# A two-layer hybrid decoder step on one core: each layer begins with tile 0's queries and keys

## What is computed

```python
def layer(x, h0, buf_a, buf_b, S0, pos, l):
    u = rmsnorm(x, norm_mix_g[l])
    a_gate, a_x, b_in, c_q, c_k, c_v, c_g = jnp.split(u @ w_in[l], splits, axis=-1)
    xa, nbuf_a = causal_dwconv(a_x, buf_a, lru_conv_w[l], lru_conv_b[l])        # 4 taps
    ha, h_last = rglru(xa, h0, ...)                                             # gates from xa
    out_a = gelu(a_gate) * ha
    glu = b_in[..., :W_B] * sigmoid(b_in[..., W_B:])
    cb, nbuf_b = causal_dwconv(glu, buf_b, cm_dw_w[l], cm_dw_b[l])              # 31 taps
    out_b = silu(layernorm_f32(cb, cm_ln_g[l], cm_ln_b[l]))
    q = rope(c_q, pos); k = rope(c_k, pos) * HD_C ** -0.5
    o, S_last = retention(q, k, c_v, S0, 128)
    out_c = silu(c_g) * groupnorm(o)
    x = x + concat([out_a, out_b, out_c]) @ w_out[l]
    return x + hier_moe(rmsnorm(x, norm_ffn_g[l]), ...)
```

## Time and profile before

| | before |
|---|---|
| timed executions | 874.23 us median, 871.57 to 878.54 |
| the profiled execution | 870.6 us, span 868.8 us |
| TensorE busy | 824.2 us, 95% |
| VectorE | 473.3 us, 54% |
| ScalarE, GpSimd | 175.6 us, 139.7 us |
| moved by DMA | 260.06 MB, mean 299 GB/s |
| chain that ended last | PE 79%, DMA 9%, DVE 5%, issue 4% |

### The profile page before, as it was taken

One profiled execution on the slowest core, in us unless ns is written; L12 is line 12 of the kernel. 1 busy time (PEld: TensorE's weight loads), 2 busy tenths in 40 slices (PEclk: granted clock), 3 DMA queues, 4 the chain that ended last, 5 costly groups with the idle time before them and its releaser, 6 DMA issues.

```text
span 868.8 us, 13634 instructions
## 1 busy us (share of the span) xinstructions
PE 824.2 (95%) x5302; PEld 469.0 (54%) x5302; DVE 473.3 (54%) x1099; ACT 175.6 (20%) x361; POOL 139.7 (16%) x193
## 2 busy tenths in 40 slices
PE   7999999999988899999899999999999879999995
PEld 6745554675545455455377445447655545545552
DVE  2468997262212377675624789954421215767666
ACT  2304123301121111111311221232112111111113
POOL 0101030011212222221010001300121113113110
PEclk9999999999999999999999999999999999999998
DMA  9890973669999999999973048347699999999961
GB/s 283 231 359 9 377 213 67 246 207 400 415 419 414 412 416 402 415 413 400 322 254 146 1 167 221 101 103 298 234 403 416 417 415 415 413 403 415 413 264 55
DMA packets 104487, 260.06 MB, mean 299 GB/s; under 512 B 34088, under 2 KB 67900, under 8 KB 87978
## 3 DMA queue, kind: packets, MB, share of 16 engines
q1 hardware_dynamic: 94954, 247.00, 75.3%
q0 software_dynamic: 7680, 9.39, 3.2%
q10 hardware_dynamic: 1792, 2.84, 0.9%
HBM read 265.22 MB, written 15.18 MB: 323 GB/s over the span
## 4 chain that ended last, share of the span: by engine, by line
PE 79%; DMA 9%; DVE 5%; issue 4%; SPq 1%; ACT 1%; POOL 0%; DVEq 0%; POOLq 0%; ACTq 0%
PE psum L1059 20%; PE psum L756 13%; PE psum L1085 11%; PE psum L735 7%; PE psum L681 6%; DMA ring<-in_moe_w 5%; PE psum L925 5%; PE psum L1114 3%; DMA rows<-xn_scratch,sg 3%; PE psum L1108 2%; PE psum L767 2%; PE psum L687 2%; DVE uT L1298 1%; PE psum L1099 1%; PE psum L1000 1%
## 5 line engine op out<-in xcount | busy, mean ns | idle before, releaser
L1059 PE MATMUL psum<-ring,arena 128*64 128x256 f32 x1984 | 227.8, 382 | 6.5 <-issue 4.6
L1059 PEld LDWEIGHTS psum<-ring,arena 128*64 128x64 f32 x1984 | 142.1, 137 | 77.5 <-issue 16.8
L1085 PE MATMUL psum<-ring,arena 128*64 128x512 f32 x496 | 118.2, 604 | 12.4 <-issue 9.0
L756 PE MATMUL psum<-ring,uT 128*128 128x512 f32 x256 | 113.0, 595 | 0.0
L1788 DVE SCALAR_TENSOR_TENSOR arena<-arena,psum 128x128 f32<-128x128 f32 x64 | 18.3, 286 | 115.9 <-ACT arena L2114 102.3
L1780 DVE TENSOR_TENSOR arena<-psum,gff 128x512 f32<-128x512 f32 x64 | 43.7, 687 | 65.6 <-PE psum L681 63.8
L756 PEld LDWEIGHTS psum<-ring,uT 128*128 128x128 f32 x256 | 47.7, 190 | 55.3 <-issue 54.5
L1085 PEld LDWEIGHTS psum<-ring,arena 128*64 128x64 f32 x496 | 36.2, 138 | 71.1 <-issue 70.0
L1834 DVE TENSOR_TENSOR x<-x,psum 128x512 f32<-128x512 f32 x80 | 51.5, 684 | 41.0 <-PE psum L1114 31.5
L2095 ACT ACTIVATE arena<-psum,sg 128x512 f32<-128x512 f32 x64 | 44.0, 688 | 128.4 <-PE psum L1085 126.1
L735 PE MATMUL psum<-uT,ring 128*128 128x288 f32 x256 | 63.1, 407 | 1.0 <-DVE uT L1298 1.0
(11 more groups left out here) (313 smaller groups left out, 912.4 us busy)
## 6 DMA issues: line engine op xcount, KB each, us to landing
ring<-in_moe_w SPq DMA_DIRECT2D x186, 1024.0 KB, 19.4
ring<-in_w_in SPq DMA_DIRECT2D x24, 1024.0 KB, 11.7
ring<-in_w_out SPq DMA_DIRECT2D x8, 1024.0 KB, 7.7
y_scratch<-in_w_out SPq DMA_DIRECT2D x1, 2304.0 KB, 18.8
arena<-in_state_ret SPq DMA_DIRECT2D x16, 128.0 KB, 5.9
out<-arena SPq DMA_DIRECT2D x16, 128.0 KB, 2.5
xn_scratch<-rows ACTq DMA_DIRECT2D x4, 512.0 KB, 3.7
uT<-in_moe_w SPq DMA_DIRECT2D x2, 1024.0 KB
```

Source lines behind the costliest of these rows:

```text
L756: i = pe.matmul(b, uTk[:, k, 128 * t:128 * t + 128], w[:, :, k, :], start=k == 0, stop=k == KT - 1)
L1059: i = pe.matmul(b[64 * j:64 * j + 64, 0:FE], xsT[:, u // 2, k, s], w[j][:, k, :], start=k == 0, stop=k == KT - 1, skip_group_check=True)
L1085: i = pe.matmul(b[64 * q:64 * q + 64, :], hT[:, q, f, :], w[:, 512 * j:512 * j + 512], start=f == 0, stop=f == 1, skip_group_check=True)
```

## The change

Each layer now begins with tile 0 alone: norm of tile 0, q0 on TensorE, and the norms of tiles 1 and 2 run beside it. Then states, (layer 0) parameters, k0, tq0, b4, tk0, b5, b6, b7 and last b0 to b3. SP loads the granules in that order, and the first experts' weights after b3 instead of b5. On VectorE the short convolution moves behind 12 taps of the long one, the samples' taps behind the first rotations; parameters stand between the rotations of q0 and k0. At a layer's end tile 0's sums come first, and the next layer's first tile (or the final norm's) is done ahead of the samples' sums, inside the branch; TensorE no longer waits for the last sums ahead of its branch.

```diff
-WAIT_NORM, WAIT_CHOICE, WAIT_MARKS, WAIT_GATES, WAIT_ROWS = (13, 8), 16, 6, 7, 7
+WAIT_NORM, WAIT_CHOICE, WAIT_MARKS, WAIT_GATES, WAIT_ROWS = (6, 5), 16, 6, 7, 7
...
             for l in range(DEPTH):
-                full(sp, l, "b5")
+                full(sp, l, "b3")
                 expert(l, 0, 0)
...
-                    for kind, u, gs in (("h", 0, (0, 1)), ("h", 1, (3, 4)), ("h", 2, (6, 7)), ("y1", 0, (2, 5))):
+                    for kind, u, gs in (("h", 1, (4, 3)), ("h", 2, (6, 7)), ("y1", 0, (5, 2, 0, 1))):
...
+                norm(l, 0, 0)
                 project("q0", 4, 0)
+                norm(l, 0, 1)
+                norm(l, 0, 2)
+                states(l)
+                if l == 0:
+
+                    pe.wait_ge(param_in, 16 * len(params))
...
                 project("k0", 6, 0)
+                turn("tq0", 0)
+                freed(pe, l, "n1t2a")
+                block(4)
+                turn("tk0", 0)
+                for c in (5, 6, 7, 0, 1, 2, 3):
+                    block(c)
                 project_samples()
...
-                    for a in (0, 2, 1, 3):
+                    for a in range(4):
                         xfreed(pe, f"y{a % 2}", 1, GROUPS - 1, l)
...
                 n = pe.value_load(ovi[0:1, 8:9], min_val=0, max_val=OVER)
-                for kind, u in (("x0", 1), ("x1", 1), ("h", 3), ("hT", 3), ("y0", 1), ("y1", 1), *((f"back{a}", 1) for a in range(5))):
-                    xfreed(pe, kind, u, GROUPS - 1, l)
                 with pe.If(n > 0):
...
+                if l == 0:
+                    dve.wait_ge(const_in, 16)
                 rotate_q(0)
+                if l == 0:
+                    parameters()
                 rotate_k(0)
-                taps(0, 9)
+                glu()
+
+                full(dve, l, "tq0")
+                taps_samples(0)
+                taps_samples(1)
+                own.wait()
+                dve.sem_inc(sample_conv, 1)
+                taps(0, 12)
+                short_conv()
...
-                given_back(NPAIR - 1, (0, 2, 1, 3, 4))
+                given_back(NPAIR - 1, (0, 1))
...
-                    dve.nop()
...
+                    given_back(NPAIR - 1, (2, 3))
+                    first_tile(l + 1)
+                    given_back(NPAIR - 1, (4,))
```

More of the change, by code:

```diff
@@ L724, in _, with project, block @@
             for l in range(DEPTH):
-                for t in range(3):
-                    norm(l, 0, t)
-                freed(pe, l, "n1t2a")
-                for c in range(8):
+                def project(name, g, t):
+                    for h in range(2):
+                        granule(pe, l, g + h, "in")
+                    b = start(l, name)
+                    w = ring[:, g:g + 2, :].rearrange("p g (k c) -> p g k c", k=KT)
+                    for k in range(KT):
+                        if name == "q0" and k % 4 == 0:
+                            freed(pe, l, ("n1t0a", "n1t0b")[k // 4])
+                        i = pe.matmul(b, uTk[:, k, 128 * t:128 * t + 128], w[:, :, k, :], start=k == 0, stop=k == KT - 1)
+                    done(i, name)
+                def block(c):
                     granule(pe, l, c // 2, "in")
                     b = start(l, f"b{c}")[:, 0:NT]
+                    if l == 0 and c == 7:
+                        pe.wait_ge(prm_ready, 1)
                     w = ring[:, c // 2, :].rearrange("p (k c) -> p k c", k=KT)
@@ L858, in _ @@
                 gates("gi1", 1, 1)
-                turn("tq0", 0)
-                turn("tk0", 0)
                 project("q1", 4, 1)
@@ L1359, in _, with short_conv @@
-                dve.wait_ge(glu_ready, 2 * l + 2)
+                def short_conv():
+                    freed(dve, l, "b3")
+                    freed(dve, l, "sa")
+                    last = [None] * 4
+                    for k in range(CONV_A):
+                        for c in range(2):
+                            w = P_(l, "cw", 2 * k + c)
+                            for i, (src, dst) in enumerate((
+                                    (axp[:, c, k:k + SEQ], pr(XA)[:, c, :]),
+                                    (axs[:, c, :, k:k + DT], sa(XA)[:, c, :, :]))):
+                                if k == 0:
+                                    ins_ = S(dst, src, w, P_(l, "cb", c), ALU.mult, ALU.add)
+                                else:
+                                    own.wait(last[2 * c + i])
+                                    ins_ = STT(dst, src, w, dst, ALU.mult, ALU.add)
+                                if k < CONV_A - 1:
+                                    last[2 * c + i] = own(ins_)
+                                elif (c, i) == (1, 1):
+                                    ins_.then_inc(xa_ready, 1)
+                                else:
+                                    own(ins_)
@@ new lines, in glu @@
+                def glu():
+                    freed(dve, l, "b7")
+                    freed(dve, l, "sc")
+                    STT(glp[:, :, 30:LB], pr(xc[:, :]), 1.0, pr(cb[:, :]), ALU.add, ALU.mult).then_inc(glu_ready, 1)
+                    dve.wait_ge(glu_ready, 2 * l + 1)
+                    for c in range(2):
+                        i = STT(gls[:, c, :, 30:LT], sa(xc[:, :])[:, c], 1.0, sa(cb[:, :])[:, c], ALU.add, ALU.mult)
+                        if c:
+                            i.then_inc(glu_ready, 1)
+                        else:
+                            own(i)
+                    dve.wait_ge(glu_ready, 2 * l + 2)
@@ L1517, in _ @@
                 dve.sem_inc(mixa_done, 1)
-                taps(12, 15)
+                taps(15, 18)
                 full(dve, l, "S0")
@@ L1525, in _ @@
                 mask_scores(2)
-                taps(15, 24)
+                taps(18, 25)
                 mask_scores(1)
@@ L1884, in _ @@
                 n = dve.value_load(ovi[0:1, 8:9], min_val=0, max_val=OVER)
[L1885 to L1886 removed]
                 with dve.If(n > 0):
+                    given_back(NPAIR - 1, (2, 3, 4))
+                    for a in range(5):
+                        xfreed(dve, f"back{a}", 1, GROUPS - 1, l)
                     with dve.Fori(0, n) as j:
```

205 lines of the change are left out of this document (86 added, 119 removed), and 1 row of the table jobs.

## The result

The changed kernel takes 879.59 us (median of 17 runs, 874.38 to 888.42), the kernel before, run beside it, 875.17 (17 runs, 870.65 to 878.54): ratio 1.0051, 95% interval 1.0031 to 1.007. That is 4.4 us slower, within the 1% that I had called no change, 5.2 us above my number of 874.4 and inside the range of 868 to 882. The profiled execution took 878.43 us with a span of 876.6, against 868.8 before, so the two traces lie 7.8 us apart.

What follows compares the result with a forecast made beforehand. TensorE was taken as the bound. Layer 0 +2.1 + 1.3, layer 1 -3.3 + 1.3 and end +0.1 gave +1.5 us; on 872.9, the middle of four executions, that made 874.4 us, range 868 to 882.

Steps and rivals of the forecast that it cites:

- The bound: Whole kernel: TensorE, busy 95% of the span, sets the time; gains or losses ahead of the experts' part carry through unchanged.
- Rival 4: Experts' part: the weight stream sets the pace and swallows any shift ahead of it, 0 +- 1 us, 874; chance 0.05.
- Layer 1's head: Start of layer 1: q0 starts 5.3 us sooner, 1.95 of transposes are paid back, net gain 3.3 us.
- Layer 0's head: Start of layer 0: no gain from the new order; low clock and the key's late rotation lose 2.1 us by q1.
- 3.6 us per MB: Loads at layer 0's start: rate from 2.62 MB in 9.6 us, putting granule 5's arrival at 12.2, say 12.5.
- The rotation of k0: Layer 0, VectorE: delayed by constants and parameters, kr done at about 35.2, and TensorE's tk0 waits for it until 35.7.
- the clock term: q0 of layer 0: the first stretch runs at the lower clock, so about 1.7 us falls into q0; bounds 0 and 6.9.
- The wait at the gates: Ahead of gr0, both layers: GpSimd's gelu slows VectorE's taps by 2.3 us, slack 1.0, so TensorE waits 1.3 us each.
- rival 3: At gr0: GpSimd holds up every tap and the short convolution, wait 3.7 us per layer, sum +6.3, 879; chance 0.18.
- Rival 2: At the gates: taps slip between GpSimd's operations without loss, no waits, sum -1.1 or to -4, 870 to 873; chance 0.27.
- The end: Kernel's end: tile 0's last normalisation moves ahead, tile 2's sums behind it; the last tile decides, +0.1 us.
- the edits that I took as free: Six tap instructions done earlier and the first experts' weights loaded after b3 instead of b5: both claimed to cost nothing.

Runs made afterwards that it cites:

- The fastest kernel: Nine ahead-taps instead of 12; layer 0 starts with blocks b4 to b7, has 26 filler passes, b3 between k0 and tq0: 868.12 us, 0.9924 of the kernel before.

## Why the prediction was right or wrong

**The bound** held. What TensorE gained or lost in a head or at the gates arrived at the end: 7.9 at layer 0's q1, 7.9 at the last give-back, 7.8 in the span. Rival 4, the weight stream that swallows a shift, is out. But single traces are not that exact: from q1 of layer 0 to the last give-back the kernels before and after take 360.9 us both, and the traces of experiments whose edits do not touch that part 360.9 to 363.2.

**Layer 1's head** was right: 5.5 us sooner against 5.3, 1.9 paid back against 1.95, net 3.6 against 3.3. That the cover by q0 is what earns it, is shown by the run that takes it away. Reading the overflow count put VectorE's third sum back by 0.4 us, as I had allowed, and cost nothing: the rows of tile 0 were ready at 440.96, and the filler held TensorE until 441.02.

**Layer 0's head** was mis-sized: +3.9 (without the gates) against +2.1. Two terms of it had the right size, transposes 1.9 and clock 1.6 (I had 1.7). Two failed. q0 started at 13.4 rather than 12.5; the arrival of granule 5 varies from 12.2 to 14.6 between profiled runs, and my 3.6 us per MB lies at the early end. And b4 waited 1.35 us for granule 2, a wait that I had not written down. My own figure would have shown it: q0 and k0 use four granules in 14 us, and at 3.6 us per MB they also arrive in some 14, with constants, states and x between them. The rotation of k0, which I had expected to release tk0, did not: it was done at 35.7 (I had "kr at about 35.2", though my terms add up to 34.9), tk0 started at 37.39, and without b4's wait TensorE would have come to it at 36.0, still behind the rotation. The reason that I gave for the clock term was wrong although its size was right: with the cold start removed q0 was as slow (8.80 us), so it goes with the idle time ahead of q0.

**The wait at the gates** had the right place, cause and layer count, and the wrong price: 4.0 and 3.8 us against 1.3 each. I had VectorE late by 1.3, measured is 2.36. The share that a GpSimd operation takes from the taps, "70%", was right: 2.45 us, 69% of the 3.56 that the gelu's operations took. Missing were 0.9 us in the short convolution (5.35 us where 4.5 are usual). 0.8 of them went in the instruction beside L2231, the scaling of the keys, which I had nowhere; GpSimd's copies, which I had in rival 3, took 0.1. And I had no term for what an idle TensorE does to its own clock, 1.7 us in layer 0 and 1.4 in layer 1, though I had priced a low clock in layer 0's head. It is the largest miss, 3.1 of the 6.3 us by which the traces differ from my sum. On the rule that I weighed there (the Trainium skill, "SBUF — State Buffer", Who interferes with whom): that a vector instruction with two SBUF inputs and a GpSimd instruction that reads SBUF exclude each other agrees with the copy of 0.43 us that took 3.44 beside the taps; the loss of the whole of GpSimd's time that I drew from it does not, the taps lost 69% of it.

**The rivals.** Rival 3, to which I gave 0.18, comes nearest: slower, by the wait at the gates. Its 879 against the 879.59 measured is luck. It had a wait of 3.7 in each layer, and measured are 2.36 of wait and 1.4 to 1.7 of clock, which it lacked; it had no larger loss in layer 0's head; and it stood on a time before of 872.9. Rival 2 is refuted by the taps of 11.24 us.

**The end** cost nothing (the last give-back of layer 1 comes 8.0 us later than before, the span is 7.8 longer; I had +0.1), and nothing shows a price of the edits that I took as free: between layer 0's q1 and the last give-back, and again between layer 1's q1 and the end, the traces of before and after differ by 0.2 us at most.

**The medians.** My sum was made for one execution and put on the middle of four. The traces say +7.8 and the medians +4.4, because the profiled run of before (870.6 us, clock 0.994) was one of its fastest. Of the 5.2 us between my 874.4 and the 879.59 measured, 2.3 are the time before, which I took as 872.9 and which was 875.17, and 2.9 are the change itself, 4.4 against 1.5. That the time lies in my range therefore does not speak for my price of the gates, which was off by 5.2 us in the traces, or for layer 0's head, off by 1.8.

## What to carry to other kernels

A wait of TensorE may have to be priced twice, once for its length (2.36 us here) and once for the products behind it that run at the lower clock (1.4 to 1.7 us); filler in the wait removed the second part only. Work that is moved closer to its consumer must be timed with the neighbour that moves along with it: here one engine's gelu followed the block it waits for into a stretch where VectorE had 1 us of slack left. And an order that is best in the steady state, with all weights loaded, may be wrong for the first layer, where it is the arrival of weights per us of products that counts; two orders, one for each layer, were 0.76% faster than the kernel before.

## What the runs showed of the hardware that I had not expected

The spread between runs of one kernel goes with TensorE's granted clock. Over 35 runs of the kernel before, 870.33 to 879.63 us, time and mean granted clock have a correlation of -0.86, and 0.001 less clock goes with 0.6 us more; its runs at 0.990 or more lie between 870.3 and 875.6, those at 0.985 or less between 875.2 and 879.6. The fastest kernel was also steadier: its six runs had clocks of 0.990 to 0.994 and a spread of 2.2 us, where the 16 runs of before beside them spread over 7.2. That this comes from fewer falls of the clock is likely, but not shown. Its lead over before is 6 us in the medians and only 2.8 in the traces (866.0 against 868.8), where the run of before had one of its highest clocks, 0.994.

The clock fell to 0.54 behind a wait of 2.36 us (in the changed kernel's gates), and to 0.50 behind a stretch in which no wait was over 0.59 us (transposes behind filler, in layer 1); it stayed at 1.00 behind a stretch of 2.30 us with 0.52 busy (the kernel with the blocks first and 12 filler passes). The Trainium skill, "TensorE: Matmul & The Clock Gate", The HAM clock gate, says that activity releases the throttle; the traces agree in kind, but two kernels with the same filler and waits of 1.75 and 1.80 us fell on different sides, so no single wait read from a trace decides it.
